# Wider projections: four k rows by 512 columns in a chunk, three full banks for a group

## The chip, the cores and the metric
One core of one Trainium2 chip runs the whole program. The metric is device time in microseconds (us) of one execution; the times before are 1462.58, 1464.21 and 1458.85, median 1462.58.

## What is computed
Two layers of a transformer over 384 tokens of 1024 features (128 prompt tokens, 256 latent tokens), all in fp32. In each layer:

```python
h = _rms(x, norm1_g) * (1 + sc1) + sh1            # sh, sc, g come from silu(cond) @ ada_w + ada_b
qa, ka, va, qs, ks, vs, qr, kr, vr, gr, ga, gs, gre = _split_in(h @ w_in)    # 1024 x 6144
o_na, o_swa, o_ret = neighbourhood attention, window attention, retention
z = sigmoid(ga) * (o_na @ w_br_na) + sigmoid(gs) * (o_swa @ w_br_swa) + sigmoid(gre) * (o_ret @ w_br_ret)
x = x + g1 * (z @ w_out)                          # 1024 x 1024
h2 = _rms(x, norm2_g) * (1 + sc2) + sh2
x = x + g2 * hierarchical_moe(h2)                 # 16 experts, two for each token
```

The change touches `h @ w_in` for the first 3072 of the 6144 columns (queries, keys, values, retention gate) and `z @ w_out`.

## The kernel before
Tokens stand in three tiles of 128. Every weight passes through `ring`, four slots of 1 MB (128 partitions x 8 x 256 fp32). One list, `ORDER`, written out in advance, fixes the order of all chunks for all engines; `SLOT` and `LOADED` follow from it. SyncE (the queue SPq) loads chunk n as soon as PE has finished chunk n - 4 (`put`, semaphore `chunk_done`). The first projection half has 12 chunks ("z") in each layer, and between two of them stands an "ada" chunk of the modulation (16 small matmuls, L536), later in the layer the second projection half ("g", L794), the branch products ("br", L838), the out projection ("out", four chunks, L853), and the experts (L922, L941).

The projections are computed in fp32r with operands split in a high and a low part, three products for each: high x high, high x low, low x high. A chunk goes through in four quarters of 512 elements a partition. ScalarE (ACT) copies a quarter to `w_hi`, rounded to fp32r (`hi_quarter`, L433); VectorE (DVE) makes `w_lo = ring - w_hi` (`lo_quarter`, L439); PE multiplies. There are two buffers of each, so ACT fills one while PE uses the other, and waits for `quarter_done` or `chunk_done`. A quarter is two k rows (of 128 features) by 256 columns. The stationary operand is a 128 x 128 block of `h_hi` or `h_lo`, the moving one is 256 columns of `w_hi` or `w_lo`:

```python
for t in range(TILES):
    for k in range(2 * q, 2 * q + 2):
        for n, (hx, wx) in enumerate(((h_hi, w_hi), (h_hi, w_lo), (h_lo, w_hi))):
            mm = pe.matmul(ps[:, b + t, 0:CH], hx[:, k, t * P:(t + 1) * P], wx[:, q % 2, k % 2, :], ...)
```

A z chunk fills half of three PSUM banks (0 to 2 and 3 to 5 in turn). DVE copies out even chunks (L1149) and ACT odd ones (L1714, the last one L1716), 3 x 256 elements, in the second quarter of the chunk after. The engines run their instructions in order, so whatever stands between two quarters on DVE or ACT (these copies, the ada rows L1062, the gate rows L1069, decay tables in layer 0) shifts the quarters behind it. After the last z chunk ACT copies it out, then makes two quarters of the first g chunk; DVE follows with its two and with an ada row copy, and PE goes on with L642.

In the out projection DVE adds chunk s - 1 to x (`x_update`, L1399, L1400, L1404) in the second quarter of chunk s, and the last chunk after its last matmul. Then ACT takes the squares of x (L1678), GpSimd the root, DVE scales (L1104), and PE transposes (L584).

GpSimd's own queue loads small tensors at the start of a layer (16 loads of `na_rpb_flat`, L1908, among them) while z chunks are loaded.

Of the kernel before, what the change touches and what calls it, by code (L numbers as in the profile page):

```python
# [21 lines left out]
P = 128  # L22
# [23 lines left out]
CH = 256  # L46
# [98 lines left out]
def build(nc, a, out):  # L145
    ctx = ExitStack()
    with ctx:
# [160 lines left out]
        zt_dve, ZD = sem("zt_dve"), Z_CHUNKS // 2  # L308
# [142 lines left out]
        def _(sp):  # L451
# [7 lines left out]
            def source(item):  # L459
# [5 lines left out]
                if kind in ("z", "g"):  # L465
                    first = item[2] * CH + (Z_COLS if kind == "g" else 0)
                    return w_in[l].rearrange("(k p) c -> p k c", p=P)[:, :, first:first + CH]
                if kind == "out":
                    return a["w_out"][l].rearrange("(k p) c -> p k c", p=P)[:, :, item[2] * CH:(item[2] + 1) * CH]
# [4 lines left out]
            def put(item):  # L474
# [10 lines left out]
                elif item[0] == "down":  # L485
                    sp.dma_start(ring[:, slot].rearrange("p k c -> p (k c)").rearrange("p (j n) -> p j n", n=D),
                                 source(item)).then_inc(slot_loaded[slot], 16)
                else:
                    sp.dma_start(ring[:, slot], source(item)).then_inc(slot_loaded[slot], 16)
# [31 lines left out]
        def _(pe):  # L521
# [82 lines left out]
            for l in range(DEPTH):  # L604
                norm_transposes(l, 0, 0 if l else 5, KT)
                for c in range(Z_CHUNKS):
                    b = 3 * (c % 2)

                    if c % 2 == 0:
                        pe.wait_ge(zt_dve, l * ZD + c // 2 + 1)  # L610
                    else:
                        pe.wait_ge(zt_act, l * ZD + c // 2 + 1)
                    if c == 1:
                        pe.wait_ge(hT_dve, l * HT + 8)
                        pe.wait_ge(hT_act, l * HT + 8)
                    for q in range(4):
                        if c == 0:
                            pe.wait_ge(split_lo, l * 4 + q + 1)
                        pe.wait_ge(wlo_ready, l * QUARTERS + (4 * c + q + 1))
                        for t in range(TILES):  # L620
                            for k in range(2 * q, 2 * q + 2):
                                for n, (hx, wx) in enumerate(((h_hi, w_hi), (h_hi, w_lo), (h_lo, w_hi))):
                                    mm = pe.matmul(ps[:, b + t, 0:CH], hx[:, k, t * P:(t + 1) * P], wx[:, q % 2, k % 2, :],  # L623
                                                   start=(k == 0 and n == 0), stop=(k == KT - 1 and n == 2))
# [220 lines left out]
                for s in range(4):  # L845
                    if s >= 2:
                        pe.wait_ge(out_read, l * 4 + (s - 1))
                    for q in range(4):
                        pe.wait_ge(wlo_ready, l * QUARTERS + 4 * (SPLIT["out"] + s) + q + 1)
                        for t in range(TILES):  # L850
                            for k in range(2 * q, 2 * q + 2):
                                for n, (zx, wx) in enumerate(((h_hi, w_hi), (h_hi, w_lo), (h_lo, w_hi))):
                                    mm = pe.matmul(ps[:, 3 * (s % 2) + t, 0:CH], zx[:, k, t * P:(t + 1) * P], wx[:, q % 2, k % 2, :],  # L853
                                                   start=(k == 0 and n == 0), stop=(k == KT - 1 and n == 2))
# [141 lines left out]
        def _(dve):  # L996
# [56 lines left out]
            for l in range(DEPTH):  # L1053
# [86 lines left out]
                for c in range(Z_CHUNKS):  # L1140
                    for q in range(4):
# [4 lines left out]
                        if q == 1:  # L1146
                            if c % 2 == 1:
                                done(("z", l, c - 1))
                                dve.tensor_copy(zt[:, :, (c - 1) * CH:c * CH], ps[:, 0:3, 0:CH]).then_inc(zt_dve, 1)  # L1149
# [244 lines left out]
                def x_update(s):  # L1394
                    done(("out", l, s))
                    b = 3 * (s % 2)
                    cols = slice(s * CH, (s + 1) * CH)
                    tmp = work[:, (s % 2) * 768:(s % 2 + 1) * 768].rearrange("p (t c) -> p t c", t=TILES)
                    link(dve.tensor_tensor(tmp[:, 0], ps[:, b, 0:CH], gb[:, 0, cols], ALU.mult))  # L1399
                    dve.tensor_tensor(tmp[:, 1:3], ps[:, b + 1:b + 3, 0:CH], bcast(gb[:, 1, cols], [P, 2, CH], 1),  # L1400
# [10 lines left out]
                for s in range(4):  # L1411
                    for q in range(4):
                        if s or q:
                            lo_quarter(dve, l, "out", s, q)
                        if s and q == 1:
                            x_update(s - 1)
# [221 lines left out]
        def _(act):  # L1638
# [41 lines left out]
            for l in range(DEPTH):  # L1680
# [25 lines left out]
                for c in range(Z_CHUNKS):  # L1706
                    for q in range(4):
# [4 lines left out]
                        if q == 1 and c and c % 2 == 0:  # L1712
# [315 lines left out]
```

## Time and profile before

| | |
|---|---|
| times of three runs | 1462.58, 1464.21, 1458.85 us |
| profiled execution, its own time | 1456.1 us |
| its span | 1454.3 us |
| PE, matmuls | 1232.8 us busy, 85% |
| PE, weight loads (beside the matmuls) | 1018.5 us, 70% |
| DVE | 528.2 us, 36% |
| ACT | 365.4 us, 25% |
| GpSimd | 141.6 us, 10% |
| DMA | 280.59 MB, mean 193 GB/s |

Busy time of matmuls is taken from start to a modelled end, and matmuls overlap, so what one costs in a stream is read from the distance of two starts. PEclk is the granted clock of TensorE, 1.0 for 2.4 GHz and 0.5 for 1.2 GHz. In a row of the timeline the bracket at the end is the idle time of the engine before the instruction and what ended it.

### The profile page before, as it was taken

The page shows a single profiled execution, that of the slowest core. Times are in us where ns is not written, and L with a number is a line of the kernel's source. Part 1 is how long each engine was busy: PE and PEld are TensorE (multiplying, and loading weights), DVE is VectorE, ACT ScalarE, POOL GpSimd, SP SyncE. Part 2 cuts the span into 40 slices and gives each one's busy share as a digit, 9 for nine tenths or more (in the row PEclk, how much of TensorE's full clock was granted, in tenths as well). Part 3 has the DMA queues.
Part 4 walks back from the last instruction along what each step waited for, and adds up shares of the span by engine and source line. Part 5 has one row for each costly group of instructions (what it writes and reads, how often), then busy time and mean ns, then how long its engine had stood idle before and what let it go on. Part 6 is the DMA issues. An engine that isn't in the chain of part 4 may idle for free.

```text
span 1454.3 us, 18385 instructions
## 1 busy us (share of the span) xinstructions
PE 1232.8 (85%) x7551; PEld 1018.5 (70%) x7551; DVE 528.2 (36%) x1165; ACT 365.4 (25%) x759; POOL 141.6 (10%) x194
## 2 busy tenths in 40 slices
PE   2599989899998769999718998989999876999970
PEld 0498968799857547777518987778995764777750
DVE  1334454433255442222153335444334544222214
ACT  2232236233312301111132222532331221111111
POOL 6000010100000021111043001000000002111102
PEclk9999988899999879999959999789999988999995
DMA  9865640066633248999948655004532224899953
GB/s 282 238 214 192 213 168 1 26 202 215 209 108 114 87 157 309 364 359 371 328 135 182 222 185 181 1 5 139 179 117 87 99 104 145 311 365 360 372 226 144
DMA packets 149445, 280.59 MB, mean 193 GB/s; under 512 B 7024, under 2 KB 121872, under 8 KB 137072
## 3 DMA queue, kind: packets, MB, share of 16 engines
q1 hardware_dynamic: 131280, 219.12, 44.1%
q0 software_dynamic: 17472, 58.66, 12.2%
q10 hardware_dynamic: 608, 1.62, 0.3%
q8 instruction: 61, 1.00, 0.3%
q14 instruction: 24, 0.20, 0.0%
HBM read 253.68 MB, written 25.69 MB: 192 GB/s over the span
## 4 chain that ended last, share of the span: by engine, by line
PE 77%; DVE 9%; DMA 6%; ACT 3%; issue 2%; POOL 1%; SPq 0%; DVEq 0%; POOLq 0%; ACTq 0%
PE ps L922 15%; PE ps L623 14%; PE ps L794 14%; PE ps L941 7%; PE ps L838 6%; PE ps L853 5%; DMA ring<-in_ada_w 3%; PE ps L536 3%; PE ps L736 2%; PE ps L910 2%; PE ps L699 2%; DMA scratch_ys<-arena 1%; PE ps L584 1%; DMA ring<-in_w_in 1%; PE ps L721 1%
## 5 line engine op out<-in xcount | busy, mean ns | idle before, releaser
L439 DVE TENSOR_TENSOR w_lo<-ring,w_hi 128x512 fp32r<-128x512 f32 x224 | 155.4, 696 | 329.9 <-ACT w_hi L433 329.9
L433 ACT ACTIVATE w_hi<-ring 128x512 fp32r<-128x512 f32 x224 | 140.8, 631 | 471.9 <-PE ps L794 182.8
L922 PE MATMUL ps<-ring,arena 128*128 128x256 f32 x1024 | 226.5, 379 | 4.0 <-ACT arena L1823 4.0
L922 PEld LDWEIGHTS ps<-ring,arena 128*128 128x128 f32 x1024 | 194.2, 190 | 43.0 <-issue 13.4
L623 PE MATMUL ps<-w_hi,h_hi 128*128 128x256 f32 x576 | 167.1, 290 | 8.1 <-DVE w_lo L439 4.8
L623 PE MATMUL ps<-w_lo,h_hi 128*128 128x256 f32 x576 | 164.3, 285 | 0.0
L623 PE MATMUL ps<-w_hi,h_lo 128*128 128x256 f32 x576 | 164.1, 285 | 0.0
L794 PE MATMUL ps<-h_hi,w_hi 128*128 128x384 f32 x384 | 133.8, 348 | 8.7 <-DVE w_lo L439 4.9
L794 PE MATMUL ps<-h_lo,w_hi 128*128 128x384 f32 x384 | 132.0, 344 | 0.0
L794 PE MATMUL ps<-h_hi,w_lo 128*128 128x384 f32 x384 | 131.7, 343 | 0.0
L623 PEld LDWEIGHTS ps<-w_hi,h_hi 128*128 128x128 f32 x576 | 111.9, 194 | 17.7 <-issue 17.6
L941 PE MATMUL ps<-ring,arena 128*128 128x512 f32 x256 | 115.6, 594 | 2.8 <-DVE arena L1568 2.8
L623 PEld LDWEIGHTS ps<-w_lo,h_hi 128*128 128x128 f32 x576 | 111.9, 194 | 0.0
L623 PEld LDWEIGHTS ps<-w_hi,h_lo 128*128 128x128 f32 x576 | 111.8, 194 | 0.0
L536 PE MATMUL ps<-ring,cond 128*32 128x256 f32 x768 | 56.5, 415 | 39.0 <-DMA ring<-in_ada_w 39.0
L794 PEld LDWEIGHTS ps<-h_hi,w_hi 128*128 128x128 f32 x384 | 74.8, 195 | 15.4 <-DVE w_lo L439 5.9
L1568 DVE COPY arena<-ps 128x256 f32<-128x256 f32 x32 | 13.6, 424 | 195.4 <-PE ps L929 195.4
L838 PE MATMUL ps<-biasT,ring 128*128 128x384 f32 x256 | 83.2, 487 | 0.6 <-DVE biasT L1352 0.6
L941 PEld LDWEIGHTS ps<-ring,arena 128*128 128x128 f32 x256 | 46.1, 190 | 49.5 <-issue 45.9
L1830 ACT ACTIVATE arena<-ps 128x256 f32<-128x256 f32 x32 | 12.3, 384 | 256.7 <-PE ps L922 256.7
L794 PEld LDWEIGHTS ps<-h_hi,w_lo 128*128 128x128 f32 x384 | 75.0, 195 | 0.0
L794 PEld LDWEIGHTS ps<-h_lo,w_hi 128*128 128x128 f32 x384 | 74.7, 195 | 0.0
(267 smaller groups left out, 1666.3 us busy)
## 6 DMA issues: line engine op xcount, KB each, us to landing
ring<-in_ada_w SPq DMA_DIRECT2D x48, 1024.0 KB, 8.3
ring<-in_w_in SPq DMA_DIRECT2D x48, 1024.0 KB, 5.3
ring<-in_w_gate SPq DMA_DIRECT2D x32, 1024.0 KB, 7.7
ring<-in_w_up SPq DMA_DIRECT2D x32, 1024.0 KB, 8.8
ring<-in_w_down SPq DMA_DIRECT2D x32, 1024.0 KB, 8.2
scratch_ys<-arena POOLq DMA_DIRECT2D x32, 512.0 KB, 8.2
ring<-in_w_out SPq DMA_DIRECT2D x8, 1024.0 KB, 5.0
gb<-in_ada_b POOLq DMA_DIRECT2D x8, 512.0 KB, 4.8
```

Source lines behind the costliest of these rows:

```text
L433: eng.activation(w_hi[:, q % 2], ring[:, slot, 2 * q:2 * q + 2, :], ACT.Copy).then_inc(whi_ready, 1)
L439: eng.tensor_tensor(w_lo[:, q % 2], ring[:, SLOT[seg, l, c], 2 * q:2 * q + 2, :], w_hi[:, q % 2].bitcast(F32), ALU.subtract).then_inc(wlo_ ...
L536: mm = pe.matmul(ps[g:g + 32, bank, (c % 2) * CH:(c % 2 + 1) * CH], cond32[:, k, :], ring[:, SLOT[item], k, :], start=(k < 4), stop=(k >= ...
L623: mm = pe.matmul(ps[:, b + t, 0:CH], hx[:, k, t * P:(t + 1) * P], wx[:, q % 2, k % 2, :], start=(k == 0 and n == 0), stop=(k == KT - 1 and ...
L699: return pe.matmul(ps[:, j, at:at + n], qkT[hp:hp + HD, qb, t * P:(t + 1) * P], k, start=True, stop=True)
L736: mm = pe.matmul(ps[:, 6 + g % 2, j * HD:(j + 1) * HD], pT[:, u % 2, c * P:(c + 1) * P], v, start=(c == 0), stop=(c == len(vs) - 1))
L794: mm = pe.matmul(ps[:, 2 * (c % 3) + j, 0:TOK], wx[:, q % 2, k % 2, j * P:(j + 1) * P], hx[:, k, :], start=(k == 0 and n == 0), stop=(k == ...
L838: mm = pe.matmul(ps[:, b + n_, 0:TOK], ring[:, s, k, (j % 2) * P:(j % 2 + 1) * P], oT[:, k, :], start=(k == k0), stop=(k == k0 + kn - 1))
L853: mm = pe.matmul(ps[:, 3 * (s % 2) + t, 0:CH], zx[:, k, t * P:(t + 1) * P], wx[:, q % 2, k % 2, :], start=(k == 0 and n == 0), stop=(k == ...
L910: mm = pe.transpose(ps[:, k // 4, (k % 4) * P:(k % 4 + 1) * P], xg[:, e % 4, k * P:(k + 1) * P], ident)
L922: mm = pe.matmul(ps[:, 2 + e % 2, w * CH:(w + 1) * CH], hgT[:, e % 2, k, :], ring[:, SLOT[name, l, e], k, :], start=(k == 0), stop=(k == K ...
L941: mm = pe.matmul(ps[:, 5 + half, :], aTs[:, e % 2, j, :], w[:, j, half * 512:(half + 1) * 512], start=(j == 0), stop=(j == 1))
```

## The change
The chunks of the first projection half and of the out projection hold four k rows by 512 columns instead of eight k rows by 256 columns: chunk 2g has k rows 0 to 3 of column group g, chunk 2g + 1 has k rows 4 to 7. The number of chunks, their 1 MB, and `ORDER` stay. A row in memory is 2 KB long instead of 1 KB. A quarter is one k row by 512 columns, still 512 elements a partition, so L433 and L439 stay. Each matmul moves 512 columns, and there are 36 of them in a chunk instead of 72. A group of two chunks fills three whole banks and is copied out once: by DVE in chunks 2, 6 and 10, by ACT in chunks 4 and 8 and after the last one, 3 x 512 elements each. In the out projection the first two chunks go to banks 0 to 2 and the last two to banks 3 to 5; x_update(0) and x_update(1) run in the second and fourth quarter of chunk 2, x_update(2) and x_update(3) after the last chunk. PE no longer waits for `out_read` inside the out projection.

```diff
--- before.py
+++ after.py
@@ -305,7 +305,7 @@
         QUARTERS = 4 * (Z_CHUNKS + G_CHUNKS + 4)
         quarter_done = sem("quarter_done")
         QD = 3 * (Z_CHUNKS + G_CHUNKS + 4)
-        zt_dve, ZD = sem("zt_dve"), Z_CHUNKS // 2
+        zt_dve, ZD = sem("zt_dve"), Z_CHUNKS // 4
         zt_act = sem("zt_act")
         kv_stored = sem("kv_stored")
         KV_L = 5 * 16
@@ -462,11 +462,13 @@
                 if kind == "ada":
                     first = item[2] * D + item[3] * CH
                     return a["ada_w"][l].rearrange("(p k) c -> p k c", k=KT)[:, :, first:first + CH]
-                if kind in ("z", "g"):
-                    first = item[2] * CH + (Z_COLS if kind == "g" else 0)
+                if kind == "g":
+                    first = item[2] * CH + Z_COLS
                     return w_in[l].rearrange("(k p) c -> p k c", p=P)[:, :, first:first + CH]
-                if kind == "out":
-                    return a["w_out"][l].rearrange("(k p) c -> p k c", p=P)[:, :, item[2] * CH:(item[2] + 1) * CH]
+                if kind in ("z", "out"):
+                    w = w_in if kind == "z" else a["w_out"]
+                    k0, first = 4 * (item[2] % 2), item[2] // 2 * 512
+                    return w[l].rearrange("(k p) c -> p k c", p=P)[:, k0:k0 + 4, first:first + 512]
                 if kind == "down":
                     return a["w_down"][l, item[2]].rearrange("(p j) c -> p j c", j=2)
                 return a["w_gate" if kind == "gate" else "w_up"][l, item[2]].rearrange("(p k) c -> p k c", k=KT)
@@ -484,6 +486,9 @@
                                      ).then_inc(slot_loaded[slot], 16)
                 elif item[0] == "down":
                     sp.dma_start(ring[:, slot].rearrange("p k c -> p (k c)").rearrange("p (j n) -> p j n", n=D),
+                                 source(item)).then_inc(slot_loaded[slot], 16)
+                elif item[0] in ("z", "out"):
+                    sp.dma_start(ring[:, slot].rearrange("p k c -> p (k c)").rearrange("p (k n) -> p k n", n=512),
                                  source(item)).then_inc(slot_loaded[slot], 16)
                 else:
                     sp.dma_start(ring[:, slot], source(item)).then_inc(slot_loaded[slot], 16)
@@ -604,24 +609,24 @@
             for l in range(DEPTH):
                 norm_transposes(l, 0, 0 if l else 5, KT)
                 for c in range(Z_CHUNKS):
-                    b = 3 * (c % 2)
-
-                    if c % 2 == 0:
-                        pe.wait_ge(zt_dve, l * ZD + c // 2 + 1)
-                    else:
-                        pe.wait_ge(zt_act, l * ZD + c // 2 + 1)
-                    if c == 1:
+                    group, b = c // 2, 3 * (c // 2 % 2)
+
+                    if c % 2 == 0 and group % 2 == 0:
+                        pe.wait_ge(zt_dve, l * ZD + group // 2 + 1)
+                    if c % 2 == 0 and group % 2 == 1:
+                        pe.wait_ge(zt_act, l * ZD + group // 2 + 1)
+                    if c == 2:
                         pe.wait_ge(hT_dve, l * HT + 8)
                         pe.wait_ge(hT_act, l * HT + 8)
                     for q in range(4):
-                        if c == 0:
-                            pe.wait_ge(split_lo, l * 4 + q + 1)
+                        k = 4 * (c % 2) + q
+                        if c < 2:
+                            pe.wait_ge(split_lo, l * 4 + k // 2 + 1)
                         pe.wait_ge(wlo_ready, l * QUARTERS + (4 * c + q + 1))
                         for t in range(TILES):
-                            for k in range(2 * q, 2 * q + 2):
-                                for n, (hx, wx) in enumerate(((h_hi, w_hi), (h_hi, w_lo), (h_lo, w_hi))):
-                                    mm = pe.matmul(ps[:, b + t, 0:CH], hx[:, k, t * P:(t + 1) * P], wx[:, q % 2, k % 2, :],
-                                                   start=(k == 0 and n == 0), stop=(k == KT - 1 and n == 2))
+                            for n, (hx, wx) in enumerate(((h_hi, w_hi), (h_hi, w_lo), (h_lo, w_hi))):
+                                mm = pe.matmul(ps[:, b + t, :], hx[:, k, t * P:(t + 1) * P], wx[:, q % 2].rearrange("p k c -> p (k c)"),
+                                               start=(k == 0 and n == 0), stop=(k == KT - 1 and n == 2))
                         mm.then_inc(quarter_done if q < 3 else chunk_done, 1)
                     if 4 <= c < 8:
                         broadcast_attn_gate(l, c - 4)
@@ -843,15 +848,14 @@
                 pe.wait_ge(br_read, l * 8 + 8)
                 pe.wait_ge(z_lo, l * 8 + 8)
                 for s in range(4):
-                    if s >= 2:
-                        pe.wait_ge(out_read, l * 4 + (s - 1))
                     for q in range(4):
+                        k = 4 * (s % 2) + q
                         pe.wait_ge(wlo_ready, l * QUARTERS + 4 * (SPLIT["out"] + s) + q + 1)
                         for t in range(TILES):
-                            for k in range(2 * q, 2 * q + 2):
-                                for n, (zx, wx) in enumerate(((h_hi, w_hi), (h_hi, w_lo), (h_lo, w_hi))):
-                                    mm = pe.matmul(ps[:, 3 * (s % 2) + t, 0:CH], zx[:, k, t * P:(t + 1) * P], wx[:, q % 2, k % 2, :],
-                                                   start=(k == 0 and n == 0), stop=(k == KT - 1 and n == 2))
+                            for n, (zx, wx) in enumerate(((h_hi, w_hi), (h_hi, w_lo), (h_lo, w_hi))):
+                                mm = pe.matmul(ps[:, 3 * (s // 2) + t, :], zx[:, k, t * P:(t + 1) * P],
+                                               wx[:, q % 2].rearrange("p k c -> p (k c)"),
+                                               start=(k == 0 and n == 0), stop=(k == KT - 1 and n == 2))
                         mm.then_inc(quarter_done if q < 3 else chunk_done, 1)
 
 
@@ -1144,9 +1148,9 @@
                         if l == 0 and q == 3 and 6 <= c < 9:
                             decay(c - 6)
                         if q == 1:
-                            if c % 2 == 1:
+                            if c % 4 == 2:
                                 done(("z", l, c - 1))
-                                dve.tensor_copy(zt[:, :, (c - 1) * CH:c * CH], ps[:, 0:3, 0:CH]).then_inc(zt_dve, 1)
+                                dve.tensor_copy(zt[:, :, (c - 2) * CH:c * CH], ps[:, 0:3, :]).then_inc(zt_dve, 1)
                             if c in (2, 4, 6, 8, 10):
                                 ada_rows(l, 2 + (c - 1) // 4, c // 2 % 2 == 0)
                             if 5 <= c < 9:
@@ -1392,12 +1396,13 @@
 
                 dve.wait_ge(gb_ready, l * GB + 4)
                 def x_update(s):
-                    done(("out", l, s))
-                    b = 3 * (s % 2)
+                    done(("out", l, s | 1))
+                    b = 3 * (s // 2)
                     cols = slice(s * CH, (s + 1) * CH)
                     tmp = work[:, (s % 2) * 768:(s % 2 + 1) * 768].rearrange("p (t c) -> p t c", t=TILES)
-                    link(dve.tensor_tensor(tmp[:, 0], ps[:, b, 0:CH], gb[:, 0, cols], ALU.mult))
-                    dve.tensor_tensor(tmp[:, 1:3], ps[:, b + 1:b + 3, 0:CH], bcast(gb[:, 1, cols], [P, 2, CH], 1),
+                    at = s % 2 * CH
+                    link(dve.tensor_tensor(tmp[:, 0], ps[:, b, at:at + CH], gb[:, 0, cols], ALU.mult))
+                    dve.tensor_tensor(tmp[:, 1:3], ps[:, b + 1:b + 3, at:at + CH], bcast(gb[:, 1, cols], [P, 2, CH], 1),
                                       ALU.mult).then_inc(out_read, 1)
                     linked()
                     dve.wait_ge(out_read, l * 4 + s + 1)
@@ -1412,8 +1417,9 @@
                     for q in range(4):
                         if s or q:
                             lo_quarter(dve, l, "out", s, q)
-                        if s and q == 1:
-                            x_update(s - 1)
+                        if s == 2 and q % 2 == 1:
+                            x_update(q // 2)
+                x_update(2)
                 x_update(3)
 
 
@@ -1709,11 +1715,11 @@
                             hi_quarter(act, l, "z", c, q)
                         if l == 0 and q == 3 and 1 <= c < 5:
                             decay(c - 1)
-                        if q == 1 and c and c % 2 == 0:
+                        if q == 1 and c and c % 4 == 0:
                             done(("z", l, c - 1))
-                            act.activation(zt[:, :, (c - 1) * CH:c * CH], ps[:, 3:6, 0:CH], ACT.Copy).then_inc(zt_act, 1)
+                            act.activation(zt[:, :, (c - 2) * CH:c * CH], ps[:, 3:6, :], ACT.Copy).then_inc(zt_act, 1)
                 done(("z", l, Z_CHUNKS - 1))
-                act.activation(zt[:, :, (Z_CHUNKS - 1) * CH:Z_COLS], ps[:, 3:6, 0:CH], ACT.Copy).then_inc(zt_act, 1)
+                act.activation(zt[:, :, (Z_CHUNKS - 2) * CH:Z_COLS], ps[:, 3:6, :], ACT.Copy).then_inc(zt_act, 1)
                 for q in range(2):
                     hi_quarter(act, l, "g", 0, q)
```

## Rows read from the trace of the kernel before

**Rows 1.** The page: engine totals (busy, share of span, count) and the chain by line.
```profile
PE 1232.8 (85%) x7551; PEld 1018.5 (70%) x7551; DVE 528.2 (36%) x1165; ACT 365.4 (25%) x759; POOL 141.6 (10%) x194
...
PE ps L922 15%; PE ps L623 14%; PE ps L794 14%; PE ps L941 7%; PE ps L838 6%; PE ps L853 5%; DMA ring<-in_ada_w 3%; PE ps L536 3%; PE ps L736 2%; PE ps L910 2%; PE ps L699 2%; DMA scratch_ys<-arena 1%; PE ps L584 1%; DMA ring<-in_w_in 1%; PE ps L721 1%
```

**Rows 2.** Chain in order of time, 84 to 95 us: start, us, what.
```profile
84.55 8.82 PE ps L623 x72
93.37 1.00 PE ps L536 x16
```

**Rows 3.** Timeline of PE, first projection: start, us, engine, line, operation, tiles, shapes, count.
```profile
100.27 0.28 PE L623 MATMUL ps<-w_lo,h_hi 128*128 128x256 f32 x1
...
102.91 0.28 PE L623 MATMUL ps<-w_hi,h_lo 128*128 128x256 f32 x1
```

**Rows 4.** Timeline of PE, second projection half (L794).
```profile
331.22 0.34 PE L794 MATMUL ps<-h_lo,w_hi 128*128 128x384 f32 x1
...
339.20 0.34 PE L794 MATMUL ps<-h_hi,w_lo 128*128 128x384 f32 x1
```

**Rows 5.** Chain in order of time, 570 to 590 us, in the experts.
```profile
574.67 3.44 PE ps L941 x8
578.11 6.91 PE ps L922 x32
```

**Rows 6.** Stretch at the start of L853: PE, PEld, DVE, ACT, POOL busy, PEclk, DMA.
```profile
449.40:452.20 2.80, 2.80 (x13) 2.80 (x14) 0.48 (x1) 0.00 (x0) 0.00 (x0) 0.50 0.05 13
```

**Rows 7.** Timeline 50 to 100 us, DVE and PE: third quarter of chunk 0.
```profile
68.36 0.69 DVE L439 TENSOR_TENSOR w_lo<-ring,w_hi 128x512 fp32r<-128x512 f32 x1
```

**Rows 8.** Timeline of DVE, chunks 2 and 3 of layer 0.
```profile
84.86 0.68 DVE L1062 COPY mrow<-ps 128x512 f32<-128x512 f32 x1
...
94.68 0.95 DVE L1149 COPY arena<-ps 128x768 f32<-128x768 f32 x1
97.42 0.69 DVE L439 TENSOR_TENSOR w_lo<-ring,w_hi 128x512 fp32r<-128x512 f32 x1 [1.78 <-ACT w_hi L433]
```

**Rows 9.** Timeline at the end of the first projection of layer 0.
```profile
185.92 0.81 ACT L1716 ACTIVATE arena<-ps 128x768 f32<-128x768 f32 x1 [3.69 <-PE ps L623]
...
189.84 2.90 PE L642 MATMUL ps<-arena,cst 128*128 128x384 f32 x4 [2.95 <-DVE mrow L1062]
```

**Rows 10.** ACT's groups by form: line, operation, shapes, count, busy, mean ns, idle.
```profile
L1714 ACT ACTIVATE arena<-ps 128x768 f32<-128x768 f32 x10 | 7.9, 793 | 0.0
...
L1810 ACT ACTIVATE work<-ps 128x1024 f32<-128x1024 f32 x6 | 5.9, 1022 | 13.6 <-PE ps L870 13.6
```

**Rows 11.** Timeline after the last out matmul of layer 0.
```profile
485.44 0.42 DVE L1399 TENSOR_TENSOR work<-ps,gb 128x256 f32<-128x256 f32 x1 [2.95 <-PE ps L853]
...
487.56 1.06 ACT L1678 ACTIVATE work<-x 128x1024 f32<-128x1024 f32 x1 [5.79 <-DVE x L1404]
...
494.36 3.00 PE L584 MATMUL ps<-cst,work 128*128 128x128 f32 x13 [8.96 <-DVE work L1104]
```

**Rows 12.** Timeline of DVE, out projection, chunk 1.
```profile
460.21 0.69 DVE L439 TENSOR_TENSOR w_lo<-ring,w_hi 128x512 fp32r<-128x512 f32 x1 [1.40 <-ACT w_hi L433]
...
462.81 0.69 DVE L439 TENSOR_TENSOR w_lo<-ring,w_hi 128x512 fp32r<-128x512 f32 x1
```

**Rows 13.** Chain in order of time, 780 to 800 us, layer 1.
```profile
771.92 13.58 DMA ring<-in_w_in
...
787.03 10.26 PE ps L623 x72
```

**Rows 14.** Timeline of PE at the start of chunk 2 of layer 1.
```profile
787.03 0.55 PE L623 MATMUL ps<-w_hi,h_hi 128*128 128x256 f32 x1 [4.31 <-DVE w_lo L439]
```

**Rows 15.** The page: DMA issues of the first projection: count, KB, median us to landing.
```profile
ring<-in_w_in SPq DMA_DIRECT2D x48, 1024.0 KB, 5.3
```

**Rows 16.** DMA queues, 772 to 786 us: packets, MB, share of 16 engines.
```profile
q1 hardware_dynamic: 2042, 2.07, 58.2%
q0 software_dynamic: 410, 0.81, 46.1%
```

## The prediction
> **What bounds the kernel now.** I read the page first. PE is busy for 85% of the span, DVE for 36%, ACT for 25%, and the chain by line is mostly PE: L623 (first projection half) and L853 (out projection), the two groups of matmuls that change, hold 14% and 5% of it [rows 1]. Then the chain in order of time, one chunk of L623: 72 matmuls in 8.82 us, then 1.00 us of the 16 matmuls of the ada chunk, then the next chunk, with nothing between [rows 2]. So in these stages the matmul rate decides, and the reader should look for what one matmul costs. The timeline of PE gives it by start times. At full clock 23 starts of a 256-column fp32r matmul stand from 100.27 to 102.91, so 2.64/22 = 120.0 ns each [rows 3]; a quarter boundary lies among them and shows no gap. The 384-column matmuls of L794 stand from 331.22 to 339.20 with 46 intervals, 173.5 ns each [rows 4]. At 2.4 GHz the columns alone take 106.7 and 160.0 ns. Left over are 13.3 and 13.5 ns: a charge per matmul that does not grow with width.
>
> **Part 1: half as many matmuls, twice as wide.** A chunk has 4 k x 3 tiles x 3 products = 36 matmuls of 512 columns instead of 72 of 256. The trace of before has no fp32r matmul of 512 columns. The nearest rows are the two above; carried on they give 213.3 + 13.4 = 226.7 ns. The bounds: the fp32 matmuls, 512 columns in 3.44/8 = 430 ns and 256 in 6.91/32 = 216 ns, take two cycles a column (426.7, 213.3) and only some 3 ns more [rows 5], so 216.5 ns is the low end; the high end is two charges, one for each 256 columns, 240 ns. I take 226.7, since it is a line through two rows of the same type. Per pair of old matmuls that saves 240.0 - 226.7 = 13.3 ns, per chunk 36 x 13.3 = 0.48 us, and over 2 x (12 + 4) = 32 chunks 15.3 us. All of it lies on the path, except: while the granted clock is 0.5 (1.2 GHz) the starts are 0.21 us apart, the columns alone, and nothing is saved; that holds for 13 matmuls at the start of L853 [rows 6] and about as many at three other starts, so 26 pairs x 13.3 = 0.35 us less. In the first chunk of a layer the third quarter begins when DVE has made w_lo (ready at 69.05, PE starts on it at once [rows 7]), which hangs on the norm and not on PE, so what the first two quarters save is lost: some 0.15 us, twice. Term: **-14.6 us**.
>
> By the Trainium skill ("TensorE: Matmul & The Clock Gate", section "Back-to-back issue gap") a warm matmul comes N / 2.4 + 2.5 ns after the one before. This trace contradicts it for fp32r at 256 and 384 columns by 10.8 ns and agrees for fp32; at 512 columns it would give 215.8 ns, an estimate from that page, and a term of about -27 us.
>
> **Part 2: evictions of three full banks.** DVE's copy grows from 3 x 256 elements, 0.95 us, to 3 x 512; at about 1.04 ns an element (L439's 512 take 0.69, the 768 take 0.95 [rows 8]) that is 1.75 us, 0.8 more. It now comes after the second w_lo of chunks 2, 6 and 10, which also have an ada row copy of 0.68. Queued behind it on DVE are w_lo of quarter 2, and PE behind that. In chunk 3 of before DVE is free from 95.63 to 97.42, 1.79 us [rows 8]; less 0.12 for PE's shorter quarter leaves 1.67 against 0.8 + 0.65 = 1.45 of new work. Hidden, by 0.2 us; and w_lo has 0.6 us more before PE would wait. Chunk 6 has another 0.65 (gate rows), but PE gets 0.9 of broadcast before it. ACT's copies in chunks 4 and 8 are hidden likewise. Not hidden is the last one of each layer: ACT's copy starts when the last chunk is done, both quarter copies of the next projection stand behind it on ACT, then DVE's w_lo and the row copy, and then PE at 189.84 after 2.95 idle [rows 9]. From 768 to 1024 elements ACT goes from 793 to 1022 ns [rows 10], 0.8 to 0.9 ns an element, so 768 more cost 0.6 to 0.7 us: **+1.2 us** for two layers.
>
> **Part 3: the out projection's updates of x.** Before, x_update(s - 1) ran on DVE under the matmuls of s, and only x_update(3) stood at the end. Now 0 and 1 run under s = 2, and 2 and 3 both stand behind the last matmul. One lasts from 485.44 until ACT's squares start at 487.56, less ACT's 0.1 to start [rows 11]: 2.0 us. PE then waits for norm and transposes, so nothing hides it: **+4.0 us** for two layers. Bounds: 1.9 to 2.1 each. PE's idle there grows from 9 to 11 us; it restarts at the low clock already. The dropped waits on out_read never showed as idle. Inside s = 2: x_update holds DVE until 462.81, and w_lo is ready at 463.50 [rows 12]. The chunk began at 459.46 (0.75 before the w_lo at 460.21), so PE wants it at 459.46 + 4.32 = 463.78 now and at 463.54 with quarters of 2.04 us. Cover of 0.04 us: I count 0.05 for each of four such places, **+0.2 us** (0 to 0.6).
>
> **Part 4: loads with rows of 2 KB instead of 1 KB.** The bytes and their order stay, SP's queue too. In layer 0 no chunk is waited for. In layer 1 one is: z chunk 2, issued at 771.92, lands 13.58 us later against a median of 5.3, PE starts at 787.03 after 4.31 idle, and its chunk takes 10.26 instead of 8.82, at the low clock at first [rows 13 to 15]. Meanwhile GpSimd's queue has 410 packets that take 46.1% of 16 engines for 14 us, 252 ns each; SP's take 64 ns [rows 16]. Were an engine to alternate between the queues packet by packet, its 64 packets of this load would meet up to 64 of the others; the slowest engine met (13.58 - 64 x 0.064) / 0.252 = 38. With 32 packets of double size it meets 32: 6 x 0.252 = 1.5 us sooner (an estimate from those rows). PE comes 0.5 us earlier and then waits that much more. So **-1.0 us**. Bounds: shared by bytes, +0.5; with the stall and its low clock gone, -(4.3 + 1.4) + 0.5 = -5.2. I stay near the small end, because DMA is full all through that stretch and the same bytes must move.
>
> **Sum.** -14.6 + 1.2 + 4.0 + 0.2 - 1.0 = -10.2 us. The profiled execution lasted 1456.1 (span 1454.3), so 1445.9. The median of the runs shown is 6.5 above it; by it, 1462.6 - 10.2 = **1452.4 us**.
>
> **Rivals.**
> *A, the charge goes at 512 columns.* For: fp32 rows pay only 3 ns [rows 5], and a weight load of 0.19 us would fit inside one matmul of 213 ns. Against: it did not shrink from 256 to 384. The price is 1152 x 10.2 ns = 11.7 us more gained: 1440.7. Chance 0.10. The rule of the skill quoted above is this rival.
> *B, the gain is eaten.* DVE's 0.04 us of cover in the out projection is not enough, or the z evictions take w_lo past its place: PE is then paced by DVE, and the chunks concerned save nothing (8 of out, 3.8 us, or 6 of z, 2.9 us), while the load of z chunk 2 lands no sooner (+1.5). One or both: 1455 to 1459, within 0.5% of before. For: the slack worked out is small. Against: DVE is only 36% busy. Chance 0.24.
> *C, slower: the wide fp32r matmul costs more than two narrow ones.* The loser is the same place, L623 and L853: if the charge at a full bank were three of 13.3, 40 ns, each matmul takes 253 ns, 1152 x 13.3 = +15.3 us, and with the +4.4 of the parts above the time is 1482. It becomes slower by over 0.5% from a charge of about 29 ns. For: no fp32r row at 512. Against: the two fp32r widths have the same charge, and fp32 at 512 shows nothing special. Chance 0.04.
> The forecast itself holds 0.62.
>
> **How the numbers follow.** What a measurement of this kernel can tell from no change is about 0.5%, 7.3 us: faster is below 1455.3, slower above 1469.9. The forecast's own range is 1447 to 1457 (part 4 from -5.2 to +0.5, run to run 2 us), and some nine tenths of it lies below 1455.3; with A that gives 0.66 faster. B, and the rest of the forecast, give 0.30 the same; C 0.04. Range 1440 to 1459: it takes in A, the forecast and B.
>
> **What would show it.** In the profile after: L623 and L853 with 288 + 96 matmuls of each of the three products, starts 0.227 us apart (A: 0.216; C: over 0.24); a chunk of z in about 8.35 us; ACT's eviction of 1536 elements at about 1.4 us and PE's idle before L642 at 3.6; two x_updates behind the last out matmul, PE's idle before L584 at about 11; the stall before z chunk 2 of layer 1 between 3 and 4 us. If PE waits for w_lo inside chunks, part 2 or 3 is wrong (B). If the stall before z chunk 2 is gone, part 4 was mis-sized and the time is near 1448.

## The result, and the profile after

The changed kernel took 1453.99 us, median of 9 runs (1447.33 to 1460.77); the kernel before, run beside it, 1462.58 us, also 9 runs. The ratio is 0.9948, with a 95% interval of 0.9924 to 0.9973: a little faster, as forecast (1452.4 us). The profiled execution lasted 1451.36 us against 1456.1, its span 1449.6 against 1454.3.

The page after, engine totals and the chain by line; they answer to [rows 1]. L628 is the former L623, L799 the former L794, L856 the former L853, L541 the former L536.

```profile
PE 1223.7 (84%) x6399; PEld 957.0 (66%) x6399; DVE 527.9 (36%) x1159; ACT 365.0 (25%) x753; POOL 141.4 (10%) x194
...
PE ps L926 15%; PE ps L799 14%; PE ps L628 13%; PE ps L945 7%; PE ps L843 6%; PE ps L856 5%; DMA ring<-in_ada_w 3%; PE ps L541 3%; PE ps L741 2%; PE ps L914 2%; PE ps L704 2%; DMA scratch_ys<-arena 1%; PE ps L647 1%; PE ps L589 1%; PE ps L726 1%
```

1152 matmuls fewer, and L628 gave up one per cent of the chain. How the rate came out is read from the timeline of PE, layer 0, between two ada chunks:

```profile
84.61 0.50 PE L628 MATMUL ps<-w_hi,h_hi 128*128 128x512 f32 x1
84.95 0.40 PE L628 MATMUL ps<-w_lo,h_hi 128*128 128x512 f32 x1
85.19 0.40 PE L628 MATMUL ps<-w_hi,h_lo 128*128 128x512 f32 x1
...
87.50 0.39 PE L628 MATMUL ps<-w_hi,h_hi 128*128 128x512 f32 x1
...
92.72 0.39 PE L628 MATMUL ps<-w_hi,h_lo 128*128 128x512 f32 x1
```

From 87.50 to 92.72 stand 23 intervals, 227 ns each; over the steady intervals of L856 at full clock the mean is 226.8. The forecast was 226.7. But the stream starts worse than it runs: the first interval is 340 ns, and the next ten or so are 230 to 240. The chain in order of time shows what that leaves of a chunk:

```profile
83.68 1.00 PE ps L541 x16
84.68 8.43 PE ps L628 x36
93.10 1.00 PE ps L541 x16
```

8.43 us against 8.82 [rows 2], so 0.39 less and not 0.48. Beyond the steady rate the 72 narrow ones lost 8.82 - 72 x 0.120 = 0.18 us, the 36 wide ones lose 8.43 - 36 x 0.2268 = 0.27. About 0.09 us of each stands at the chunk's end, before the ada matmuls start (0.32 us from the last start instead of 0.23, and 0.21 instead of 0.12); the rest is the restart, 0.17 us wide and 0.09 narrow.

The end of the first projection (answers to [rows 9]), timeline of three engines:

```profile
181.91 1.45 ACT L1722 ACTIVATE arena<-ps 128x1536 f32<-128x1536 f32 x1 [3.45 <-PE ps L628]
...
185.63 0.68 DVE L1066 COPY mrow<-ps 128x512 f32<-128x512 f32 x1
...
186.46 1.62 PE L647 MATMUL ps<-arena,cst 128*128 128x384 f32 x2 [3.59 <-DVE mrow L1066]
```

ACT's copy grew from 0.81 to 1.45 us and PE's idle time from 2.95 to 3.59: all of the growth lands on the path. The end of the out projection (answers to [rows 11]):

```profile
482.59 0.42 DVE L1404 TENSOR_TENSOR work<-ps,gb 128x256 f32<-128x256 f32 x1 [2.72 <-PE ps L856]
...
484.59 0.42 DVE L1404 TENSOR_TENSOR work<-ps,gb 128x256 f32<-128x256 f32 x1
...
486.70 1.06 ACT L1684 ACTIVATE work<-x 128x1024 f32<-128x1024 f32 x1 [7.56 <-DVE x L1409]
...
493.51 4.52 PE L589 MATMUL ps<-cst,work 128*128 128x128 f32 x24 [10.96 <-DVE work L1108]
```

Two updates of x stand behind the last matmul, 2.00 us apart, and PE idles 10.96 us instead of 8.96. Inside chunk 2 the update now holds DVE just too long:

```profile
468.38 0.96 DVE L1409 SCALAR_TENSOR_TENSOR x<-work,x 128x768 f32<-128x768 f32 x1
469.26 0.69 DVE L439 TENSOR_TENSOR w_lo<-ring,w_hi 128x512 fp32r<-128x512 f32 x1
```

w_lo is ready at 469.95. PE's starts are 469.64 and then 470.00 and 470.34, where 0.23 apart would be the rate: some 0.13 us of waiting and 0.11 of restart, and in all of chunk 2 0.27 us.

The stall before z chunk 2 of layer 1 (chain in order of time, answers to [rows 13]) is smaller in this execution, by 1.1 us of landing time:

```profile
769.29 12.48 DMA ring<-in_w_in
...
783.29 10.04 PE ps L628 x36
```

That this is the longer rows' doing is not shown. The out-only kernel of the second experiment below still loads its z chunks in rows of 1 KB, and its chain has for the same load:

```profile
780.82 12.89 DMA ring<-in_w_in
```

Where the 4.7 us of the span came from, by the first and last starts of each stage in the two profiled executions (after less before, us; the last column sums both layers):

| stage | layer 0 | layer 1 | sum |
|---|---|---|---|
| up to the first matmul of the projection | +0.72 | | +0.7 |
| first projection half, first to last start | 122.28 to 117.43, -4.85 | 127.58 to 122.23, -5.35 | -10.2 |
| to the out projection (the longer copy +0.64 in it) | +1.23 | +1.51 | +2.7 |
| out projection, first to last start | -0.06 | -1.57 | -1.6 |
| last out matmul to the transposes | +2.11 | +2.11 | +4.2 |
| the rest of the layer | -1.61 | +1.04 | -0.6 |

The out projection of layer 0 gained nothing because its start fell into 6.2 us of granted clock 0.5 instead of 2.9; there the starts are 427 ns apart, which is 512 columns at 1.2 GHz and nothing more. The stages that the change does not touch moved by up to 1.6 us. Part of it goes with the time at granted clock 0.5 (between the first projection and the out projection of layer 0, 41.6 us instead of 38.1); in layer 1 that time is the same there (37.6 and 37.5), and what moved stays open.

### The profile page after: what moved, and what is told of

Same layout as the page of the kernel before. It is cut to its first block, busy times and chain, and to the rows that moved or that the text cites. A ratio compares the mean times of both kernels' runs of the same rounds, so it can differ in the third digit from the quotient of the medians.

```text
span 1449.6 us, 16061 instructions
## 1 busy us (share of the span) xinstructions
PE 1223.7 (84%) x6399; PEld 957.0 (66%) x6399; DVE 527.9 (36%) x1159; ACT 365.0 (25%) x753; POOL 141.4 (10%) x194
## 3 DMA queue, kind: packets, MB, share of 16 engines
q0 software_dynamic: 17472, 58.66, 12.3%
## 4 chain that ended last, share of the span: by engine, by line
PE 76%; DVE 9%; DMA 6%; ACT 4%; issue 3%; POOL 1%; SPq 0%; DVEq 0%; POOLq 0%; ACTq 0%
PE ps L926 15%; PE ps L799 14%; PE ps L628 13%; PE ps L945 7%; PE ps L843 6%; PE ps L856 5%; DMA ring<-in_ada_w 3%; PE ps L541 3%; PE ps L741 2%; PE ps L914 2%; PE ps L704 2%; DMA scratch_ys<-arena 1%; PE ps L647 1%; PE ps L589 1%; PE ps L726 1%
## 5 line engine op out<-in xcount | busy, mean ns | idle before, releaser
L439 DVE TENSOR_TENSOR w_lo<-ring,w_hi 128x512 fp32r<-128x512 f32 x224 | 155.4, 696 | 325.6 <-ACT w_hi L433 325.6
L433 ACT ACTIVATE w_hi<-ring 128x512 fp32r<-128x512 f32 x224 | 140.9, 631 | 464.1 <-PE ps L799 182.9
L926 PEld LDWEIGHTS ps<-ring,arena 128*128 128x128 f32 x1024 | 194.2, 190 | 43.0 <-issue 13.4
L799 PE MATMUL ps<-h_hi,w_hi 128*128 128x384 f32 x384 | 133.9, 349 | 8.7 <-DVE w_lo L439 4.9
L799 PE MATMUL ps<-h_lo,w_hi 128*128 128x384 f32 x384 | 131.8, 343 | 0.0
L799 PE MATMUL ps<-h_hi,w_lo 128*128 128x384 f32 x384 | 131.5, 342 | 0.0
L628 PE MATMUL ps<-w_hi,h_hi 128*128 128x512 f32 x288 | 116.7, 405 | 8.0 <-DVE w_lo L439 4.5
L628 PE MATMUL ps<-w_hi,h_lo 128*128 128x512 f32 x288 | 113.5, 394 | 0.0
L628 PE MATMUL ps<-w_lo,h_hi 128*128 128x512 f32 x288 | 113.4, 394 | 0.0
L541 PE MATMUL ps<-ring,cond 128*32 128x256 f32 x768 | 56.5, 415 | 40.0 <-DMA ring<-in_ada_w 40.0
L799 PEld LDWEIGHTS ps<-h_hi,w_hi 128*128 128x128 f32 x384 | 74.6, 194 | 15.4 <-DVE w_lo L439 5.9
L1836 ACT ACTIVATE arena<-ps 128x256 f32<-128x256 f32 x32 | 12.3, 384 | 256.7 <-PE ps L926 256.7
L799 PEld LDWEIGHTS ps<-h_lo,w_hi 128*128 128x128 f32 x384 | 74.8, 195 | 0.0
L799 PEld LDWEIGHTS ps<-h_hi,w_lo 128*128 128x128 f32 x384 | 74.8, 195 | 0.0
L628 PEld LDWEIGHTS ps<-w_hi,h_hi 128*128 128x128 f32 x288 | 55.0, 191 | 29.0 <-issue 15.1
L843 PEld LDWEIGHTS ps<-biasT,ring 128*128 128x128 f32 x256 | 48.4, 190 | 34.4 <-DVE biasT L1356 0.8
L589 PE MATMUL ps<-cst,work 128*128 128x128 f32 x96 | 18.5, 377 | 57.9 <-DVE work L1108 57.9
```

Source lines behind the costliest of these rows:

```text
L433: eng.activation(w_hi[:, q % 2], ring[:, slot, 2 * q:2 * q + 2, :], ACT.Copy).then_inc(whi_ready, 1)
L439: eng.tensor_tensor(w_lo[:, q % 2], ring[:, SLOT[seg, l, c], 2 * q:2 * q + 2, :], w_hi[:, q % 2].bitcast(F32), ALU.subtract).then_inc(wlo_ ...
L541: mm = pe.matmul(ps[g:g + 32, bank, (c % 2) * CH:(c % 2 + 1) * CH], cond32[:, k, :], ring[:, SLOT[item], k, :], start=(k < 4), stop=(k >= ...
L589: mm = pe.transpose(ps[:, k, t * P:(t + 1) * P], xn[:, t, k * P:(k + 1) * P], ident)
L628: mm = pe.matmul(ps[:, b + t, :], hx[:, k, t * P:(t + 1) * P], wx[:, q % 2].rearrange("p k c -> p (k c)"), start=(k == 0 and n == 0), stop ...
L799: mm = pe.matmul(ps[:, 2 * (c % 3) + j, 0:TOK], wx[:, q % 2, k % 2, j * P:(j + 1) * P], hx[:, k, :], start=(k == 0 and n == 0), stop=(k == ...
```

## The experiments

All ratios are to the kernel before, run on the same chip in the same rounds.

**Which half of the change pays.** The first projection alone:

```diff
-                if kind in ("z", "out"):
+                if kind == "z":          # w_out, L853, x_update as before
```

> Only the first projection half is changed; the out projection is as before. My theory: all the net gain is here. Per z chunk 0.39 us (36 matmuls 226.4 ns apart instead of 72 at 119.8, as the profile after shows), 24 chunks: -9.4; +1.3 for ACT's last eviction of 1536 elements, twice; -1 for z chunk 2 of layer 1. Sum about -9 us against before (ratio 0.994), and no second x_update in the tail: PE idle before L584 at about 9 us. Rival: the out projection carries its share of the gain (8 of 32 chunks), then this one gains only three quarters of what both do, -5 to -6 us, and is slower than the changed kernel.

Measured: 1453.49 us, ratio 0.9950 (0.9922 to 0.9979). It is level with the whole change (0.9948). The out projection alone (the first projection as before):

```diff
-                if kind in ("z", "out"):
+                if kind == "out":        # w_in, L623 and its copies as before
```

> Only the out projection is changed. My theory: it brings nothing. 8 chunks x 0.45 = -3.6 us, +4.0 for the second x_update behind the last matmul, +0.5 for DVE being late with w_lo inside chunk 2: about +1 us against before (ratio 1.000 to 1.002). In the profile, PE idle from the last out matmul to L584 is 11 us instead of 9, and two starts of about 350 ns in chunk 2. Rival: the tail is covered by something else, then -3 us (0.998).

Measured: 1464.53 us, ratio 1.0035 (1.0008 to 1.0063): a small loss. All of the net gain is the first projection's. The two ratios do not quite add up to the whole change's: together they give 0.9985, and its interval ends at 0.9973. The section on the clock takes this up.

**Is it the width of the matmul?** All of the change, but each 512-column matmul is issued as two of 256 columns:

```diff
-  mm = pe.matmul(ps[:, b + t, :], hx[...], wx[:, q % 2].rearrange("p k c -> p (k c)"), ...)
+  for half in range(2):
+      for n, (hx, wx) in enumerate(...):
+          mm = pe.matmul(ps[:, b + t, half * CH:(half + 1) * CH], hx[...], wx[:, q % 2, half, :], start=True, stop=True)
```

> The changed kernel with each 512-column matmul issued as two of 256 columns, 72 in a chunk again; layout, loads of 2 KB rows, evictions and x_updates are the changed kernel's. Each matmul opens and closes its own sum, so the products are not added up over k. My theory (a charge of 13.3 ns for each matmul): starts 119.8 ns apart, the whole gain of the matmuls goes, 1152 x 13 = +14 us against the changed kernel, so about +5 us against before (ratio 1.003). Rival: the gain came from the longer rows in memory and the fewer evictions; then the time stays at the changed kernel's (0.995).

This kernel leaves out the sum over k, so its output is not the projection; its loads, copies and waits are the changed kernel's. Measured: 1463.81 us, ratio 1.0031 (1.0007 to 1.0055). Its chain has the old chunk back:

```profile
84.73 8.82 PE ps L629 x72
```

So the rows of 2 KB, the full banks and the fewer copies bring nothing; what they cost together is the loss that was forecast for them (+1.2, +4.0, +0.2, -1.0). The gain is the wide matmul's. What no run separates: each matmul here comes with a weight load of its own (6399 of each after, 7551 before), so half the matmuls are half the weight loads too, and the charge of 13.4 ns may belong to either.

**The stall and the small loads.** The whole change, and GpSimd's loads of `na_rpb_flat` wait for a z chunk each pair, instead of going out together:

```diff
+                        pool.wait_ge(chunk_done, SEQ["z", l, 1 + (rp * HEADS_NA + h) // 2] + 1)
                         pool.dma_start(...)      # na_rpb_flat, L1908
```

> The changed kernel, but GpSimd issues the 16 bias loads of a layer two at a time, each pair after one more z chunk (chunks 1 to 8), instead of all at once at the start of the layer. My theory: z chunk 2 of layer 1 lands late only because these loads share the DMA engines; it lands 6 to 8 us after its issue instead of 12.5, PE's idle of 3.6 us before it goes and with it the low clock at its start (1.6 us): -5 us against the changed kernel (ratio 0.991 against before), nothing in layer 0. Rival: the other loads at the start of the layer (gate rows, caches) or SyncE's own ada loads hold it up; then the stall stays at 3 us or more. Second rival: the spread loads hold up a later z chunk by as much.

Measured: 1438.46 us, ratio 0.9843 (0.9799 to 0.9887), far more than expected. The stall before z chunk 2 is gone (chain in order of time, layer 1: one chunk follows the other):

```profile
760.75 8.43 PE ps L628 x36
769.17 1.00 PE ps L541 x16
770.17 8.44 PE ps L628 x36
```

The rest came from a place that I had not looked at: the start of the program, where PE waits for the modulation's weights. To see whether it belongs to the change at all, the kernel before got the same line:

```diff
+                        pool.wait_ge(chunk_done, SEQ["z", l, 1 + (rp * HEADS_NA + h) // 2] + 1)
                         pool.dma_start(...)      # L1908 of the kernel before
```

> The kernel before, with only the loads of na_rpb_flat spread over the z chunks as in e4. Theory (the GpSimd loads slow the weight loads at the start of a layer, whatever the shape of the chunks): the start-up of layer 0 shortens by some 8 us and the stall before z chunk 2 of layer 1 (4.3 us and 1.4 at the low clock) goes, so about 1446, ratio 0.990. Rival (the wide chunks are needed for it: rows of 2 KB stand better beside the small loads): no more than the stall goes, ratio 0.996 or above.

Measured: 1442.31 us, ratio 0.9892 (0.9866 to 0.9918). The DMA queues from 5 to 50 us, first of the kernel before, then of this one (q1 is SyncE's, q0 GpSimd's; packets, MB, share of 16 engines):

```profile
q1 hardware_dynamic: 8110, 8.51, 66.7%
q0 software_dynamic: 1536, 3.64, 34.5%
```

```profile
q1 hardware_dynamic: 11180, 11.60, 82.9%
q0 software_dynamic: 768, 2.06, 18.2%
```

and its chain there, where the kernel before has 43.46 us for the same two loads:

```profile
5.47 35.07 DMA ring<-in_ada_w x2
40.54 0.04 issue
40.58 1.94 PE ps L536 x16
```

The engines are full in both. GpSimd's loads are small but their packets are not (2.4 KB each on average, SyncE's 1.05 KB); they take a third of the engines' time and carry 3.64 of 12.8 MB. With the sixteen loads of `na_rpb_flat` put off, half of q0's packets and half of its share go over to the loads that PE waits for. The first projection begins at 55.17 us instead of 63.33, and in layer 1 it lasts 122.01 instead of 127.58; in layer 0 it lasts 1.5 us longer (2.4 in the fourth experiment), since the spread loads now hold up z chunks there (7 to 11 us to land instead of 5.3). PE waits for w_lo 1.43 us once here, and 1.42, 0.24 and 0.50 us in the fourth experiment, so the second rival of the fourth is there too, in small. The theory holds, and it is independent of the change.

**Can the two losses be taken back?** As the fourth experiment, with the out projection as before the change:

```diff
-                if kind in ("z", "out"):
+                if kind == "z":          # w_out, L853, x_update as before; the loads spread
```

> As e4, but the out projection as before the change. If the out part of the change costs what the second experiment showed (ratio 1.0035, +5 us), this is 1 to 5 us faster than e4: ratio 0.981 to 0.984. If that loss came only with the other low-clock stretches, it is level with e4, 0.984 to 0.987.

Measured: 1440.27 us, ratio 0.9888 (0.9853 to 0.9923). The interval shuts out the first expectation and leaves part of the second: it isn't shown faster than the fourth, and not shown slower either, for the intervals overlap. In its profiled execution, the slowest of its six (1451.70 us), the out projections and what follows are 2.7 us shorter than in the fourth (91.2 against 93.9), as they should be, but the first projection of layer 0 lasts 123.38 against 119.78, with late z chunks and 9.4 us at granted clock 0.5 in it against 3.4.

Then half and half: out chunks 0 and 1 wide, chunks 2 and 3 narrow, so that only the last update of x stands in the tail:

```diff
+                if s < 2:   # 512 columns, one k row a quarter, banks 0 to 2
+                else:       # 256 columns, two k rows a quarter, banks 3 to 5 and 0 to 2
...
-                x_update(2)
                 x_update(3)
```

> As e4, but the out projection holds its first two chunks wide (512 columns, one group) and its last two narrow (256 columns, eight k rows), so that x_update(2) goes back under the last chunk. Against e4: 2.0 us less in each tail (-4.0), 0.25 less wait in chunk 2 (-0.5), half of the wide matmul's gain lost (+1.8): some -2.7 us, ratio about 0.982. Rival: DVE is now behind in chunk 3 or the low clock takes it back; level with e4.

Measured: 1433.73 us, ratio 0.9869 (0.9830 to 0.9909). Its timeline of DVE behind the last out matmul has one update, as before:

```profile
472.70 0.42 DVE L1414 TENSOR_TENSOR work<-ps,gb 128x256 f32<-128x256 f32 x1 [2.96 <-PE ps L867]
...
479.39 2.08 DVE L1118 TENSOR_SCALAR work<-x,rstd 128x1024 f32<-128x1024 f32 x3 [4.61 <-POOL rstd L1897]
```

Out projection and what follows take 44.47 us in each layer, against 46.99 and 46.90 in the fourth; some 1.3 us of each difference is the clock at the start (3.4 us at 0.5 against 6). So the profile shows some 1.2 us a layer from the new shape; the interval is too wide to tell the whole time from the fourth's, and at equal low clock (table below) the two are level.

Last, the copy behind the last z chunk shared by two engines, with the ada row copy ahead of the next w_lo:

```diff
-                act.activation(zt[:, :, ...], ps[:, 3:6, :], ACT.Copy).then_inc(zt_act, 1)
+                act.activation(zt[:, 0:1, ...], ps[:, 3:4, :], ACT.Copy).then_inc(zt_act, 1)
...
+                dve.tensor_copy(zt[:, 1:3, ...], ps[:, 4:6, :]).then_inc(zt_dve, 1)
+                ada_rows(l, 4, 1)        # then the two lo_quarter of the next projection
```

> As e7, and the last copy of the z groups is shared, one tile by ScalarE and two by VectorE, with the ada row copy ahead of the two w_lo of the next projection. PE's idle time behind the last z chunk (3.6 us) should fall to 2.0 to 2.8 in each layer: -1.6 to -3.2 us against e7, ratio about 0.980. Rival: the wait for w_lo of the next projection takes its place and nothing changes.

Measured: 1430.79 us, ratio 0.9812 (0.9780 to 0.9844), the lowest time of all; its interval still touches those of the fourth and the seventh. The timeline at the end of its first projection:

```profile
176.04 0.60 ACT L1736 ACTIVATE arena<-ps 128x512 f32<-128x512 f32 x1 [3.45 <-PE ps L631]
```

```profile
176.04 1.22 DVE L1174 COPY arena<-ps 128x1024 f32<-128x1024 f32 x1 [2.72 <-PE ps L631]
177.18 0.68 DVE L1077 COPY mrow<-ps 128x512 f32<-128x512 f32 x1
...
178.01 5.40 PE L650 MATMUL ps<-arena,cst 128*128 128x384 f32 x16 [1.00 <-DVE mrow L1077]
```

The idle time fell from 3.59 to 1.00 us in each layer, more than I had expected. This run changes two things, the shared copy and the place of the row copy, and no run separates them. The timelines speak for the second: PE waited for the row copy on DVE, which stood behind two w_lo (1.80 us) in the kernel after and stands ahead of them here. ACT's whole copy, 1.45 us long, started at 176.04, would have ended at 177.49, before the row copy does here at 177.86 (an estimate from these rows), so sharing it may have brought nothing.

**Reading small differences through the clock.** Over the 106 runs of the two rounds of experiments (those of the kernel before among them), the time goes with the time that the granted clock stood at 0.5, that is 2 x (1 - mean clock) x span: 0.30 us for each us (error 0.01), and around those lines the runs scatter by 1.9 us. Much of what differs lies in one stage, the attention (L704 to L741). Here are two executions there, the kernel after and the fourth experiment (us; PE, PEld, DVE, ACT, POOL busy; PEclk; DMA):

```profile
906.50:923.60 17.10, 16.54 (x77) 12.82 (x78) 7.72 (x36) 8.08 (x35) 0.00 (x0) 0.50 0.00 1
```

```profile
891.70:932.60 40.90, 39.83 (x187) 33.54 (x188) 14.73 (x69) 18.73 (x70) 0.00 (x0) 0.50 0.00 1
```

Put to 220 us of low clock, the kernels stand to before as follows (us, with the standard error):

| kernel | as measured (mean) | at equal low clock |
|---|---|---|
| first projection only | -7.0 | -8.5 ± 0.7 |
| out projection only | +5.5 | +1.3 ± 0.7 |
| narrow matmuls in the new layout | +4.8 | +5.5 ± 0.7 |
| change, loads spread | -20.9 | -19.0 ± 0.9 |
| before, loads spread | -14.7 | -12.0 ± 1.0 |
| first projection only, loads spread | -15.1 | -15.9 ± 1.0 |
| out half wide, loads spread | -20.4 | -18.9 ± 1.0 |
| and the shared copy | -27.0 | -23.9 ± 1.0 |

The ratios of the first two experiments now fit the whole change: -8.5 and +1.3 make -7.2, where its ratio gives -7.6. This is a way of reading, not a proof: a kernel could bring its own low clock. The out-only kernel had 236.6 us of it (± 3.6) against 222.6 (± 2.5), while the narrow one with the same tail had 220.4, so the longer idle time in the tail doesn't explain it; its cause stays open. One row doesn't add up, that of the first projection with spread loads: before with spread loads and the first projection's 8.5 would give -20.5, not -15.9, and adding the out projection to it takes off 3.1 us, where alone it costs 1.3.

## Why the prediction was right

**Part 1, the wide matmul: right, but 2 us too large.** The charge per matmul is 13.5 ns at 512 columns as at 256 and 384 (226.8 ns; forecast 226.7), so the line through two widths held, and rivals A (216) and C (over 240) fell with the first rows. The rule of the Trainium skill ("TensorE: Matmul & The Clock Gate", "Back-to-back issue gap"), which would give 215.8 ns, isn't borne out for fp32r here. The section calls it the gap of an isolated matmul and gives some 131 ns at 512 columns for a stream with weight loads, which isn't borne out either. Mis-sized was the step from the rate to the chunk: I took 36 x 13.3 = 0.48 us, and a chunk behind an ada chunk gained 0.39, because restart and end of a chunk cost 0.27 us with wide matmuls and 0.18 with narrow ones. Over 24 z chunks that is 2.0 us; the out chunks have no ada chunk between them and show the full gain (layer 1: 4 x 0.48 less the 0.27 lost in chunk 2 makes 1.65, and the stage is 1.57 shorter). On the chip, the first two kernels together (-7.2) less the narrow one (+5.5) make the wide matmul worth 12.7 ± 1.2 us at equal low clock, where 14.6 was forecast and 12.6 is what the restart leaves.

**Part 2: right.** The six copies of DVE (1.75 us) and the four of ACT (1.44) are hidden: no wait for w_lo in the chunks where they stand. The last one costs 0.64 a layer (forecast 0.6).

**Part 3: right.** The second update in the tail costs 2.0 us a layer. The cover of 0.04 us was gone, as feared, once a layer: 0.27 us in chunk 2, against 0.1 forecast. Together they eat the out projection's 3.8 us of gain: +0.6 by my terms, +1.3 ± 0.7 by the runs at equal low clock; as measured its ratio gives +1.2 to +9.2 us, and the difference is the low clock, whose cause is open.

**Part 4: not shown.** In the profiled pair the landing is 1.1 us shorter (forecast 1.5) and the idle time before the chunk 3.60 us against 4.31. But the out-only kernel, with rows of 1 KB, shows 12.9 us and 3.62, and the two others with rows of 2 KB 12.3 and 3.40 (first projection only) and 13.0 and 3.72 (narrow matmuls). What one execution differs from the next is as large as the term, so the packet by packet sharing that the prediction assumed is neither shown nor refuted. But I read only the stall: the same two queues shared the engines at the start of the program, for 43 us on the critical path, and there lay as much as the change brought. The chain by line had shown it, `in_ada_w` at 3% [rows 1], and I did not follow it, since the change doesn't touch it.

**Rival B** was half there: DVE became late in one out chunk of each layer and took 0.27 of its 0.48 us; in the z chunks it did not.

**The sum.** With the terms as measured it is -12.6 + 1.3 + 4.0 + 0.5 and, at most, -0.7 for the stall: -7.5 us where -10.2 was forecast. The ratio gives -7.6 (-3.9 to -11.1), the profiled pair -4.7. So the signs and the path were right, and part 1 was mis-sized; that the median came within 1.6 us of the forecast is in part luck, for the medians move by as much from run to run.

## What to carry to other kernels

A fixed charge per matmul can be read from two widths of the same type and carried to a third; but price the chunk, not the matmul, and look at the first ten starts after every change of shape. Work moved from under the matmuls to behind the last one costs its full duration: widen the first groups of a projection and leave the last ones narrow (shown here in the profile alone). Before tuning the stream, follow the chain's few per cent of DMA: sixteen small loads on another queue, put off by one wait, were worth more than the change.

## What the hardware showed that I had not expected

- A 512-column fp32r stream that follows the small matmuls of L541 starts with an interval of 340 ns, then ten or so of 230 to 240, before it settles at 227. After a wait of 0.13 us inside a chunk it does the same (340, then 230).
- The attention stage, which no kernel here changes, had single stretches at granted clock 0.5 of 10.2 us in one execution and of 41 us in another; at 0.30 us for each that is some 9 us of time.
- Two queues that keep the DMA engines full share them so that GpSimd's sixteen 96 KB loads hold back SyncE's 1 MB loads: at the start of the program the bytes moved went from 284 to 319 GB/s when the sixteen were put off, and the two loads that PE waits for took 35.07 us instead of 43.46.
